# Turning attention weights by transposes, with the sums spread afterwards, in a Trainium2 kernel of three transformer blocks

## The reference

```
sc = jnp.concatenate([s_loc, s_ctx, s_sink], axis=-1)     # second block
p = jax.nn.softmax(sc, axis=-1)
o = (jnp.einsum('bnkgqs,bnskd->bnqkgd', p[..., :nloc], vb)
     + jnp.einsum('bnkgqc,bckd->bnqkgd', p[..., nloc:nloc + lc], v_ctx))
...
p = jax.nn.softmax(jnp.concatenate([s_loc, s_ctx], axis=-1), axis=-1)   # third block
```

```
xf * jax.lax.rsqrt(jnp.mean(xf * xf, axis=-1, keepdims=True) + EPS) * g * (1.0 + scale) + shift
```

## Time and profile before

| what | us |
|---|---|
| median of 3 runs (lowest, highest) | 2406.17 (2405.99, 2408.24) |
| the profiled execution, its own time | 2403.84 |
| its span | 2402.0 |
| TensorE busy | 2318.0 (97%) |
| VectorE busy | 1480.0 (62%) |
| ScalarE busy | 921.2 (38%) |
| GpSimd busy | 249.1 (10%) |
| mean granted clock of TensorE | 0.982 |

### The profile page before, as it was taken

The page is one execution under the profiler, slowest core; times in us unless marked ns, Lnnn a source line. Parts: engine busy times, 40 slices in busy tenths (PEclk is TensorE's granted clock), DMA queues, the critical chain, the costliest instruction groups (busy, mean ns, idle before and its releaser), DMA issues.

```text
span 2402.0 us, 33724 instructions
## 1 busy us (share of the span) xinstructions
PE 2318.0 (97%) x14400; PEld 2015.2 (84%) x14400; DVE 1480.0 (62%) x1930; ACT 921.2 (38%) x1351; POOL 249.1 (10%) x235
## 2 busy tenths in 40 slices
PE   8999998889999999999989999999999999998999
PEld 7999895779998888888858888888888888878999
DVE  6584447577768776756765876424754333865544
ACT  6653336444454222224453322223422222544442
POOL 0030000101111101010010101100000101201110
PEclk9899998899999999999999999999999999999999
DMA  6444371255643544532202455222544322522553
GB/s 226 175 167 162 115 242 62 97 202 197 257 170 131 210 177 174 210 123 106 97 14 105 146 205 201 93 84 97 211 164 187 140 97 87 168 71 74 192 192 106
DMA packets 34834, 356.23 MB, mean 148 GB/s; under 512 B 3981, under 2 KB 6188, under 8 KB 8444
## 3 DMA queue, kind: packets, MB, share of 16 engines
q1 hardware_dynamic: 31788, 343.61, 38.6%
q0 software_dynamic: 2896, 10.46, 1.6%
HBM read 351.08 MB, written 1.13 MB: 147 GB/s over the span
## 4 chain that ended last, share of the span: by engine, by line
PE 89%; DVE 7%; ACT 3%; issue 1%; DMA 0%; POOL 0%; POOLq 0%; SPq 0%; DVEq 0%; ACTq 0%
PE psum L834 26%; PE psum L835 26%; PE psum L836 25%; PE psum L1126 2%; PE psum L882 1%; PE psum L883 1%; PE psum L884 1%; DVE ring_r L1825 1%; PE psum L1151 1%; DVE rr L1835 1%; PE psum L1121 1%; PE psum L1184 1%; PE psum L1095 1%; PE psum L1032 1%; PE psum L1023 1%
## 5 line engine op out<-in xcount | busy, mean ns | idle before, releaser
L834 PE MATMUL psum<-arena_r 128*128 128x256 f32 (+1 forms) x3384 | 1128.8, 334 | 20.5 <-DVE zT_r L1865 8.3
L836 PE MATMUL psum<-arena_r,ring_r 128*128 128x256 f32 (+1 forms) x3384 | 1119.3, 331 | 0.0
L835 PE MATMUL psum<-zT_r,arena_r 128*128 128x256 f32 (+1 forms) x2656 | 861.7, 324 | 0.0
L1351 ACT ACTIVATE arena_r<-ring 128x2048 fp32r<-128x2048 f32 (+1 forms) x252 | 473.5, 1880 | 705.8 <-PE psum L836 685.4
L834 PEld LDWEIGHTS psum<-arena_r 128*128 128x128 f32 x3384 | 637.2, 188 | 95.1 <-issue 21.8
L836 PEld LDWEIGHTS psum<-arena_r,ring_r 128*128 128x128 f32 x3384 | 639.3, 189 | 68.3
L1825 DVE TENSOR_TENSOR ring_r<-ring,arena_r 128x2048 fp32r<-128x2048 f32 (+1 forms) x252 | 568.3, 2257 | 195.5 <-ACT arena_r L1351 194.8
L835 PEld LDWEIGHTS psum<-zT_r,arena_r 128*128 128x128 f32 x2656 | 503.7, 190 | 45.1
L835 PE MATMUL psum<-arena_r 128*128 128x256 f32 (+1 forms) x1304 | 423.5, 325 | 0.0
L1976 DVE CUSTOM_DVE_ANT_0 psum<-arena,cb 128x1024 f32<-128x1024 f32 x256 | 318.1, 1302 | 0.0
L835 PEld LDWEIGHTS psum<-arena_r 128*128 128x128 f32 x1304 | 245.9, 189 | 20.4
(11 more groups left out here) (282 smaller groups left out, 1990.5 us busy)
## 6 DMA issues: line engine op xcount, KB each, us to landing
ring<-in_wf SPq DMA_DIRECT2D x75, 2048.0 KB, 7.9
ring<-in_w SPq DMA_DIRECT2D x41, 2048.0 KB, 7.9
arena<-in_w SPq DMA_DIRECT2D x72, 1024.0 KB, 9.8
ring<-in_wf SPq DMA_DIRECT2D x10, 1536.0 KB, 6.6
ring<-in_w SPq DMA_DIRECT2D x5, 1024.0 KB, 5.4
arena<-strip_scratch POOLq DMA_DIRECT2D x1, 2048.0 KB, 9.5
arena<-rpb_scratch POOLq DMA_DIRECT2D x16, 128.0 KB, 11.1
xT<-in_x SPq DMA_DIRECT2D x1, 1024.0 KB, 6.0
```

The source lines that it names most:

```text
L834: mm(b[c][:, at], whc, xh[:, k, at], start=(k == ks[0]), stop=False)
L835: mm(b[c][:, at], whc, xl[:, k, at], start=False, stop=False)
L836: last = mm(b[c][:, at], wlc, xh[:, k, at], start=False, stop=(k == ks[-1]))
L1351: A(W_hi[h % NHI][:, 0:n], ring[:, half_slot(h)], ACT.Identity).then_inc(sig("w_hi"), 1)
```

## The change

1. In `ev` and `od` a batch is turned by a transpose of the unscaled exponentials against the identity, as in `nsa`. It waits for the unit's four exponentials (`att_exp`) and no longer for the diagonal. The output of the unit is then unscaled.
2. New: `spread_sums()` on TensorE, ahead of a unit's last product. Four matmuls of a 128 x 64 matrix of ones with the diagonal of head 2j+a put 1/sum of each query on all 64 partitions of its head, in bank 4. ScalarE copies the 256 columns to `att_sums(u)`, and `att_done(u)` on VectorE is now a product of the output with them in place of a copy. The diagonals of odd units go to `rr`.
3. VectorE's order in `ev` and `od`: the finished unit's output first, then the maxima of the next unit's second half, then the diagonal, then the maxima of the unit after.
4. In `nsa` units with t = 1 the next unit's second maxima stand between the scaling of the first segment and that of the second.
5. ScalarE: in the first unit of `ev` too the next unit's exponentials come behind the copies (`parts_behind` of 1, 2, 3, 3), as in `od`.
6. In the four tails the additions of the context's squares 4 and 5 stand between the last two `c_part`.

```diff
--- before.py
+++ after.py
@@ -426,6 +426,14 @@
             at = (4 if g < 2 else 7) * BANK + (g % 2) * S
             return psum[:, at:at + S]
 
+        def att_sums(u):
+            return rt[:, S * (u % 2):S * (u % 2) + S]
+
+        def att_diag(u):
+            if u % 2:
+                return rr[:, :].rearrange("p (r t) -> p r t", r=4)
+            return E_diag if UNITS[u][0] == "ev" else O_diag
+
         def own(u, a, b):
             return small[:, 48 * (u % 2) + a:48 * (u % 2) + b]
 
@@ -1107,8 +1115,10 @@
                 def turn(i):
                     seg, blk = bs[i]
                     gb = gb0 + i
-                    if blk == bs[0][1]:
+                    if kind == "nsa" and blk == bs[0][1]:
                         pe.wait_ge(sig("att_p"), scaled_before(u) + seg + 1)
+                    if kind != "nsa" and i == 0:
+                        pe.wait_ge(sig("att_exp"), 4 * (u + 1))
                     if gb >= 2:
                         pe.wait_ge(sig("att_copied"), gb - 1)
                     pt = psum[:, (5 + gb % 2) * BANK:(6 + gb % 2) * BANK]
@@ -1117,13 +1127,8 @@
                             at = 2048 + (2 * (r % 2) + r // 2) * CMP_N if seg == 2 else place(seg, r) * S + blk * P
                         else:
                             at = r * BANK + blk * P
-                        if kind == "nsa":
-                            last = nc.tensor.transpose(pt[0:keys(i), r * P:(r + 1) * P], Pb[:, at:at + keys(i)],
-                                                       C("ident"))
-                        else:
-
-                            diag = (E_diag if kind == "ev" else O_diag)[:, r, :]
-                            last = mm(pt[:, r * P:(r + 1) * P], Pb[:, at:at + P], diag, start=True, stop=True)
+                        last = nc.tensor.transpose(pt[0:keys(i), r * P:(r + 1) * P], Pb[:, at:at + keys(i)],
+                                                   C("ident"))
                     last.then_inc(sig("att_turned"), 1)
 
                 def multiply(i):
@@ -1152,12 +1157,24 @@
                                       start=(i == 0), stop=(i == len(bs) - 1), skip_group_check=True)
                     last.then_inc(sig("att_mult"), 1)
 
+                def spread_sums():
+                    pe.wait_ge(sig("att_p"), scaled_before(u) + 1)
+                    diag = att_diag(u)
+                    for j in range(2):
+                        for a in range(2):
+                            at = 4 * BANK + j * P
+                            last = mm(psum[64 * a:64 * a + 64, at:at + P], C("ones")[:, 0:HD], diag[:, 2 * j + a, :],
+                                      start=True, stop=True)
+                    last.then_inc(sig("att_spread"), 1)
+
                 for i in range(len(bs)):
                     turn(i)
                     if i == min(2, len(bs) - 1):
                         between()
                     if i >= 1:
                         multiply(i - 1)
+                if kind != "nsa":
+                    spread_sums()
                 multiply(len(bs) - 1)
 
             def attention(u0, u1, Pb, PT, ready, beside=None, free_banks=None):
@@ -1665,7 +1682,7 @@
                     att_exp(u0, Pb, part)
                 for u in range(u0, u1):
                     n = len(batches(u))
-                    if u == u0 and beside is not None:
+                    if u == u0 and UNITS[u][0] != "nsa":
                         parts_behind = (1, 2, 3, 3)
                     else:
                         parts_behind = (-1, -1, min(1, n - 2), min(2, n - 1))
@@ -1675,6 +1692,9 @@
                         for part in range(4):
                             if parts_behind[part] == i and u + 1 < u1:
                                 att_exp(u + 1, Pb, part)
+                    if UNITS[u][0] != "nsa":
+                        act.wait_ge(sig("att_spread"), u - NSA_U[1] + 1)
+                        A(att_sums(u), psum[:, 4 * BANK:4 * BANK + S], ACT.Identity).then_inc(sig("att_spread_in"), 1)
 
 
             for i in range(2):
@@ -1937,10 +1957,12 @@
                 def between(k):
                     if k == 3:
                         c_part(6)
+                        add_square(q, 4, HALF_TOK[1], 1)
+                        add_square(q, 5, HALF_TOK[1], 1)
                         c_part(7)
 
                 z_parts(q, 0, between)
-                for m in range(4, KT):
+                for m in range(6, KT):
                     add_square(q, m, HALF_TOK[1], 1)
                 w_lo(h + 3)
                 if q == 8:
@@ -2337,7 +2359,7 @@
                         ins = v.tensor_tensor(out=own(u, 28 + 2 * a, 30 + 2 * a), in0=sink, in1=nma, op=ALU.add)
                     ins.then_inc(sig("att_max"), 1)
 
-            def att_norm(u, Pb, y):
+            def att_norm(u, Pb, y, middle=None):
                 kind, g, t = UNITS[u]
                 sm = own(u, 16, 28)
                 Pb = Pb[u % 2]
@@ -2363,6 +2385,8 @@
                         v.tensor_tensor(out=ps, in0=ps, in1=gs, op=ALU.mult).then_inc(sig("att_p"), 1)
                         if seg == 0 and u > NSA_U[0]:
                             att_done(u - 1, y)
+                        if seg == 0 and middle is not None:
+                            middle()
                     pc = Pb[:, 2048:2108].rearrange("p (r c) -> p r c", r=4)
                     link(v.tensor_tensor(out=pc, in0=pc, in1=rep(small[:, 44:48], CMP_N), op=ALU.mult))
                     va = C("valid_c").rearrange("p (t c) -> p t c", t=2)[:, t, :]
@@ -2371,14 +2395,8 @@
                 if kind == "ev":
                     link(v.tensor_tensor(out=sm[:, 0:4], in0=sm[:, 0:4], in1=own(u, 32, 36), op=ALU.add))
                 link(v.reciprocal(small[:, 36:40], sm[:, 0:4]))
-                first = (EV_U if kind == "ev" else OD_U)[0]
-                if u > first:
-                    dve.wait_ge(sig("att_turned"), batches_before(u))
-
-                v.tensor_tensor(out=E_diag if kind == "ev" else O_diag, in0=b3(C("ident"), 4, P),
+                v.tensor_tensor(out=att_diag(u), in0=b3(C("ident"), 4, P),
                                 in1=rep(small[:, 36:40], P), op=ALU.mult).then_inc(sig("att_p"), 1)
-                if u > first:
-                    att_done(u - 1, y)
 
             def att_done(u, y):
                 kind, g, t = UNITS[u]
@@ -2387,9 +2405,14 @@
                     k = 4 + 2 * g
                 else:
                     k = 2 * g
-                v.tensor_copy(y[:, k:k + 2, t * P:(t + 1) * P],
-                              psum[:, 7 * BANK:7 * BANK + 2 * P].rearrange("p (j t) -> p j t", j=2))\
-                    .then_inc(sig("att_out"), 1)
+                out, o = y[:, k:k + 2, t * P:(t + 1) * P], psum[:, 7 * BANK:7 * BANK + 2 * P]
+                o = o.rearrange("p (j t) -> p j t", j=2)
+                if kind == "nsa":
+                    v.tensor_copy(out, o).then_inc(sig("att_out"), 1)
+                else:
+                    dve.wait_ge(sig("att_spread_in"), u - NSA_U[1] + 1)
+                    v.tensor_tensor(out=out, in0=o, in1=att_sums(u).rearrange("p (j t) -> p j t", j=2), op=ALU.mult)\
+                        .then_inc(sig("att_out"), 1)
 
             def attention(u0, u1, Pb, y, beside=None, behind=None):
                 att_max(u0, (0, 1))
@@ -2398,11 +2421,19 @@
                 else:
                     att_max(u0 + 1, (0,))
                 for u in range(u0, u1):
-                    att_norm(u, Pb, y)
+                    kind = UNITS[u][0]
+                    second = (lambda: att_max(u + 1, (1,))) if u + 1 < u1 else None
+                    inside = kind == "nsa" and UNITS[u][2] == 1
+                    if kind == "nsa":
+                        att_norm(u, Pb, y, second if inside else None)
+                    elif u > u0:
+                        att_done(u - 1, y)
                     if u == u0 and beside is not None:
                         att_max(u0 + 1, (0,))
-                    if u + 1 < u1:
-                        att_max(u + 1, (1,))
+                    if second is not None and not inside:
+                        second()
+                    if kind != "nsa":
+                        att_norm(u, Pb, y)
                     if u + 2 < u1:
                         att_max(u + 2, (0,))
                     if behind is not None and u in behind:
```

## The result

| | before | after |
|---|---|---|
| median, us (lowest to highest) | 2406.08 (2405.98 to 2408.24) | 2382.62 (2381.78 to 2385.83) |
| profiled execution, its span | 2402.0 | 2380.0 |
| attention two, from the first 64-column matmul (L1256; after: L1273) to the first large matmul behind it | 63.96 | 52.80 |
| attention three, from L1301 (after: L1318) to the same | 46.01 | 38.49 |

A forecast was written before the change was run, and what follows sets the result against it. TensorE, busy in 97% of the span, was taken as the bound. Attention two -10.4, attention three -7.5, attention one +0.2 and tails -3.2 sum to -20.9 us: 2406.17 becomes 2385.3, range 2380.0 to 2392.5.

The forecast's parts named there:

- Turning: Attentions two and three: transposes make turned pairs 1.09 instead of 2.05, singles 0.66 instead of 1.16; 11.7 and 7.8 us less.
- the layout: Hand schedule of three engines' instructions with row durations and every wait; attention two ends 10.5 us earlier.
- The spreading: Four new fp32 matmuls per unit, 0.57 us each unit: 4.5 us more in attention two, 2.3 in attention three.
- The waits: TensorE's waits in attention two fall from 8.3 to 5.8 us, as turns no longer wait for the diagonal.
- Attention three: 7.8 us less turning, 2.3 more spreading, plus changed waits, with the same half-clock stretch: 7.5 us less.
- The tails: Two additions moved into a VectorE gap in four tails: 0.77 + 0.90 + 0.75 + 0.75, 3.2 us less.
- The cover: TensorE's 1.6 us wait for VectorE's L1825 at each tail's end exceeds the gain; without it, additions are worth 0.
- Attention one: Maxima between the two segments' scalings in three units: 0.2 us more, bounds 0 and +0.7.
- B: Clock falls once or twice more in attention two, costing 2 to 3 us: 2388 to 2391; chance 0.18.
- C: Waits for copies or diagonals in attentions two and three take 6 to 13 us of gain: 2391 to 2398; chance 0.12.
- D: Transposes keep attentions two and three at half clock, so slower than before, +30 us: 2436; chance 0.03.
- E: Attention three's clock fall goes (3 us) or next stages start with less waiting: 2380 to 2383; chance 0.09.

The follow-up runs named there:

- the identity kernel: Changed kernel with batches of attentions two and three turned by an fp32 matmul with the identity instead of a transpose; ratio 0.9949 to the kernel before.
- the second eight: Records added when the changed kernel's four spreading matmuls were made twice in each unit; ratio 0.9909 to the kernel before.
- attentions_only: Changed kernel without the edit of the tails and with attention one's old order of maxima; ratio 0.9922 to the kernel before.
- tails_only: Kernel before with only the two additions of squares moved in the four tails; ratio 0.9969 to the kernel before.
- scores_earlier: Changed kernel with scores behind the second turned batch, not the third, except in an attention's first unit; run twice, 0.9876 and 0.9906 to the kernel before.

## Why the prediction was right, point by point

**Right as a whole**: 2385.3 forecast, 2382.6 measured, inside the range. Part of how close the whole came is luck, since the untouched stages cancelled; the edited ones give 21.7 where 20.9 was forecast.

**Turning** (11.7 less in attention two): the records of turned batches were 25.6 us before and are 14.0 after, 11.6 less. What it is worth in the stage was left to the layout: 6.8 by the identity kernel, since behind the faster turn the waits are 3.1 longer and the scores' rows 1.0.

**The spreading is the term that was mis-sized.** I priced it at 0.57 per unit, 4.5 in attention two, from 64 records of the same tile in 4.54 us (0.071 each). From start to start eight cost 0.43 (0.054 each). The tile was the same, the order was not. The spreading goes from one half of the output's partitions to the other with each matmul, and its records start in pairs, 7 ns apart, a pair every 109 ns; the 64 make four matmuls on one half before they change, and most of their records start 52 to 109 ns apart. Of the second eight, 3.4 us in eight units by this, 2.1 showed in the stage. The first eight stand where the last product was waiting for its copy anyway: I had counted that at five places with 0.16, so 4.5 - 0.8 = 3.7 net. Leaving three quarters out won 0.65, from which I estimate the whole at about 1 us.

**The waits** in attention two were to go from 8.3 to 5.8; the profile lists 4.3. The spreading's waits are 0.6 (1.3 forecast), the scores' 1.0 (1.6), the copies' 2.4 (2.9), the first turn's 0.3 (none).
```profile
1216.51 0.70 PE L1095 MATMUL psum<-arena 64*128 64x256 f32 x4
```

```profile
1213.41 1.36 PE L1103 MATMUL psum<-arena 64*128 64x256 f32 x4
```

The heads run one behind the other at four pairs of the stage (near 1209, 1213, 1222 and 1227). So the scores lose 1.0 + 2.3 where the layout had 1.6, and this took back a part of what the spreading gave. The errors are opposite, and the stage came out at 11.1 in place of 10.4. Two slips of the working are small: the layout's 10.5 went into the sum as 10.4, and ScalarE had made two of the second unit's four exponentials ahead of the first copy, not all.

**Attention three**: 7.5, as forecast, between the first two traces. The fall of the clock is in it in every trace, and where it begins is worth over a microsecond. With the fall at about the same place in both kernels it is 7.5 (7.1 and 6.8 us into the stage: 46.01 and 38.49) and 7.1 (4.2 in both: 44.66 and, in attentions_only, 37.53). With unlike places it is 6.2 (44.66 and 38.49), so that the agreement to 0.1 is partly luck.

**The tails**: 0.85 each where 0.77, 0.90, 0.75, 0.75 were forecast. In the first, the additions left behind the low parts take 0.80 in place of 1.72, and the last residual addition starts 0.07 later; I had 0.90 and 0.13. The cover was as told: TensorE's wait was longer than the gain. That it shows 1.06 and not 0.74 left is mostly because TensorE reached it sooner. Before, it also waited 0.15 for the additions ahead of its last two matmuls on the squares; after, not:

```profile
1113.09 0.70 PE L813 MATMUL psum<-rr,cst 128*128 128x256 f32 x2 [0.15 <-DVE rr L1835]
```

```profile
1113.65 0.59 PE L821 MATMUL psum<-rr,cst 128*128 128x256 f32 x2
```

**Attention one**: +0.2 forecast, 0 to +0.3 seen.

**The rivals.** B, another fall of the clock in attention two: not in the profiles of the changed kernel, but it exists, beginning in the stage's first unit. It was there in tails_only (3.4 us, +0.7), which turns by matmuls, and in attentions_only (6.8 us, +1.9) and scores_earlier (3.4 us, +0.1 against its second trace), which transpose. So a fall there doesn't need transposes; whether they make it more frequent wasn't shown. Its price is below the 2 to 3 that I gave it. C didn't happen beyond what the layout held: waits fell. D fell: 52.8 us of attention two, turned by transposes, at a granted clock of 1.00. Here the trace disagrees with the Trainium skill, "TensorE: Matmul & The Clock Gate", "Part 4: PE-mode transpose", by which the full clock does not engage for transposes. E's case, the fall in attention three gone, was in no trace.

**What stays open**: why the two additions in the tails gave 4.8 us or more by the ratio of whole runs and 3.4 by the trace; runs of the kernel before reached from 2400.3 to 2410.9 on that chip, by clock and pace, and such a difference can come from them, but this wasn't shown for these runs. Open too is how the 4.3 us of attention two divide between the late scaling and ScalarE's new order in the first unit.

## What to carry to other kernels

Price an inserted group of small matmuls by start to start and from a row with the same order of output halves, and ask what the instruction behind it would have waited for: work put in front of a wait is nearly free. Scaling the output after the product instead of the weights before it takes the sum, the reciprocal and the diagonal out of the chain ahead of the turn; with the new orders of ScalarE and VectorE, and less the spreading, it was worth 4.3 us here beside the 6.8 of the cheaper transpose. When whole runs differ by several microseconds with no edit, compare stages between fixed landmarks: attention two, at full clock, repeated to 0.04 us. Where a stage holds a fall of the clock, compare traces that have it at the same place. And look at busy rows too: a pair of matmuls that used to run side by side can lose time without any idle time.

## What the runs showed of the hardware that was not expected

The large matmuls of a stretch run at one of two paces, 115.5 or 117.8 ns from start to start, at a granted clock of 1.00 in both; a pace holds for tens of microseconds, and the same kernel has the one in one execution and the other in the next. Over the 250 us between attention one and 704 us the second trace of before is 1.5 us longer than its first, and the first of the changed kernel 1.6. What sets it is open. Fp32 matmuls with 64 columns out run side by side when each goes to the other half of the partitions than the one ahead of it: the spreading's records start in pairs 7 ns apart, eight in 0.43 us, against 0.57 by the row of 64. The same holds for the scores, whose two heads read different halves: 0.70 us for four records side by side, 1.36 one behind the other. The stretches of half clock in the first 130 us add to 23.9 us in the first trace of before and 13.6 in the second; its start to 361 us was 2.7 us shorter.
